# Where VectorE's side work, the maxima's turn and the turns of q and k stand in an attention job

## The reference

```python
for l in range(2):
    proj = x @ w_in[l]
    o_a = chunked attention, 9 chunks of 64 keys, learned relative bias      # 4 heads
    o_b = sliding window of 2 chunks, a learned sink per head                # 4 heads
    o_c = (softmax(s1) - lam * softmax(s2)) @ v, then RMS norm per head      # 4 heads, two maps each
    o_d = attention over the top 256 keys that an indexer chooses            # 4 heads
    x = layer_norm(alpha * x + concat(o_a, o_b, o_c, o_d) @ w_out[l])
    x = layer_norm(alpha * x + square(relu(x @ w_up[l])) @ w_down[l])
```

## Time and profile before

| | us |
|---|---|
| median of 3 runs | 2806.63 (2802.84 to 2807.35) |
| the profiled execution | 2810.08 |
| its span, first to last instruction | 2808.3 |
| TensorE matmuls busy | 2697.7 (96%) |
| VectorE busy | 1670.5 (59%) |
| ScalarE busy | 976.7 (35%) |
| GpSimd busy | 1283.9 (46%) |
| chain that ended last | PE 84%, DVE 10%, DMA 2% |

### The profile page before, as it was taken

How to read it: one execution, slowest core, us unless ns; L and a number is a source line. 1 busy time by engine, 2 the same in 40 slices (tenths; PEclk the granted TensorE clock), 3 DMA queues, 4 the chain that set the end, 5 groups by cost and what they waited for, 6 DMA issues and landing times.

```text
span 2808.3 us, 36228 instructions
## 1 busy us (share of the span) xinstructions
PE 2697.7 (96%) x12768; PEld 2111.0 (75%) x12768; DVE 1670.5 (59%) x3364; ACT 976.7 (35%) x2011; POOL 1283.9 (46%) x1186
## 2 busy tenths in 40 slices
PE   8999999999999999999989999999999999999996
PEld 7788557668788888888777875676787888888885
DVE  3787776635644445544959867766364534345549
ACT  2466444442222212222225655443322222212231
POOL 5433700015665556665555345001156566556562
PEclk9999899999999999999999989999999999999998
DMA  5312334523310111110342132355323111111102
GB/s 153 86 48 56 70 80 90 130 106 94 117 45 20 60 61 61 57 44 27 96 135 55 46 80 47 76 109 117 113 90 106 57 32 32 60 60 60 57 19 101
DMA packets 98570, 207.41 MB, mean 74 GB/s; under 512 B 14138, under 2 KB 23290, under 8 KB 98106
## 3 DMA queue, kind: packets, MB, share of 16 engines
q1 hardware_dynamic: 88952, 177.68, 23.4%
q10 hardware_dynamic: 9440, 27.43, 2.7%
HBM read 142.24 MB, written 8.61 MB: 54 GB/s over the span
## 4 chain that ended last, share of the span: by engine, by line
PE 84%; DVE 10%; DMA 2%; issue 1%; SPq 1%; ACT 1%; ACTq 0%; POOL 0%; DVEq 0%
PE ps L1202 8%; PE ps L1203 8%; PE ps L1204 8%; PE ps L1089 8%; PE ps L1227 7%; PE ps L1226 7%; PE ps L1228 6%; PE ps L882 4%; PE ps L884 4%; PE ps L883 4%; PE ps L1137 2%; PE ps L1135 2%; PE ps L1136 2%; DVE x L1905 1%; PE ps L1031 1%
## 5 line engine op out<-in xcount | busy, mean ns | idle before, releaser
L838 POOL TENSOR_TENSOR wlo<-wraw,whi 128x512 fp32r<-128x512 f32 (+2 forms) x368 | 491.2, 1335 | 249.1 <-ACT whi L1287 227.2
L836 POOL CAST whi<-wraw 128x512 fp32r<-128x512 f32 (+2 forms) x272 | 184.0, 676 | 737.9 <-DMA wraw<-in_w_out 295.1
L1202 PE MATMUL ps<-xhi,whi 128*128 128x512 f32 x1024 | 406.7, 397 | 3.5 <-DVE xlo L1555 3.5
L1203 PE MATMUL ps<-xlo,whi 128*128 128x512 f32 x1024 | 406.6, 397 | 0.0
L1204 PE MATMUL ps<-xhi,wlo 128*128 128x512 f32 x1024 | 406.4, 397 | 0.0
L1976 DVE TENSOR_TENSOR common<-common,ps 128x512 f32<-128x512 f32 x104 | 69.6, 687 | 458.1 <-PE ps L1228 457.6
L1227 PE MATMUL ps<-wlo,op_hi 128*128 128x512 f32 x784 | 311.4, 397 | 0.0
L1226 PE MATMUL ps<-whi,op_hi 128*128 128x512 f32 x784 | 309.4, 395 | 0.0
L1228 PE MATMUL ps<-whi,op_lo 128*128 128x512 f32 x784 | 308.4, 393 | 0.0
L1423 ACT ACTIVATE probT<-ps 128x512 f32<-128x512 f32 (+2 forms) x456 | 204.8, 456 | 251.8 <-PE ps L1060 78.6
L838 POOL TENSOR_TENSOR wlo<-down_raw,whi 128x512 fp32r<-128x512 f32 x168 | 226.0, 1349 | 98.7 <-ACT whi L1287 92.0
(11 more groups left out here) (234 smaller groups left out, 5481.8 us busy)
## 6 DMA issues: line engine op xcount, KB each, us to landing
wraw<-in_w_up SPq DMA_DIRECT2D x144, 256.0 KB, 3.0
down_raw<-in_w_down SPq DMA_DIRECT2D x112, 256.0 KB, 3.6
wraw<-in_w_in SPq DMA_DIRECT2D x80, 256.0 KB, 2.7
slot<-q_part SPq DMA_DIRECT2D x72, 256.0 KB
slot<-k_part SPq DMA_DIRECT2D x72, 256.0 KB
wraw<-in_w_out SPq DMA_DIRECT2D x64, 256.0 KB, 2.8
wraw<-in_w_down SPq DMA_DIRECT2D x32, 256.0 KB, 2.6
slot<-q_part SPq DMA_DIRECT2D x48, 128.0 KB
```

Of the source, the lines that this page charges most:

```text
L838: nc.gpsimd.tensor_tensor(wlo[j][:, 0:w], loaded, whi[j][:, 0:w].bitcast(F32), ALU.subtract).then_inc(S["w_lo"], 1)
L1202: mm(ps[:, b, :], wh, xhi[:, k, tok], start=(k == 0), stop=False)
L1203: mm(ps[:, b, :], wh, xlo[:, k, tok], start=False, stop=False)
```

## The change

It makes four edits.

1. `between` moves from `total - 4` to `total - 3`. In 12-step jobs that is step 9, where VectorE does it behind `take_output`; in B jobs step 6, one step behind the output of step 5.
2. The maxima's turn moves from `total - 3` to `total - 4`, and within a step from the front to a place behind `turn_qk` (TensorE) and `take_turn` (ScalarE), ahead of `turn_out`.
3. A q/k turn may no longer stand at `total - 6` to `total - 4`. The turns then stand as follows (unlisted ones stay): (1,6), (1,10) become (1,10), (2,0); (5,6) becomes (5,10); (7,6), (7,10) become (7,10), (8,0); (8,6), (8,10) become (8,10), (9,0); (10,6), (10,10) become (10,10), (11,0); (11,6), (11,10), (12,0), (12,2) become (11,10), (12,0), (12,2), (12,6); (15,3), (15,7), (16,1) become (15,6), (16,1), (16,3).
4. The squares of C's norm are split: tokens 0 to 511 in job 8 and the rest in job 10, and the root moves from job 10 to job 11.

```diff
 def between_at(n):
     j, g, total = at_step(n)
-    return j + 1 < len(JOBS) and g == total - 4
+    return j + 1 < len(JOBS) and g == total - 3
 def max_turn_at(n):
     j, g, total = at_step(n)
-    return j + 1 < len(JOBS) and g == total - 3
+    return j + 1 < len(JOBS) and g == total - 4
+def pair_turn_allowed(n):
+
+    j, g, total = at_step(n)
+    return not total - 6 <= g <= total - 4 and not {n - TURN_LAG, n + 1 - TURN_LAG} & set(HALF_OF)
...
-            if n >= last + 2 and not max_turn_at(n) and not {n - TURN_LAG, n + 1 - TURN_LAG} & set(HALF_OF):
+            if n >= last + 2 and pair_turn_allowed(n):
...
             for n in range(N_STEPS + LAG):
-                if max_turn_at(n):
-                    turn_max(at_step(n)[0] + 1)
                 if n < N_STEPS:
                     score_t(n)
...
                 if pair_turn_at(n):
                     turn_qk(*pair_turn_at(n))
+                if max_turn_at(n):
+                    turn_max(at_step(n)[0] + 1)
                 if n - TURN_LAG in HALF_OF:
                     turn_out(HALF_OF[n - TURN_LAG])
...
             for n in range(N_STEPS + LAST_STEPS):
-                if max_turn_at(n):
-                    take_max(at_step(n)[0] + 1)
                 if n < N_STEPS:
                     exponent(n)
                 if pair_turn_at(n):
                     take_turn(*pair_turn_at(n))
+                if max_turn_at(n):
+                    take_max(at_step(n)[0] + 1)
...
-                if job == 8:
-                    square_c(0)
-                    square_c(4)
-                if job == 10:
+                if job in (8, 10):
+                    square_c(0 if job == 8 else 4)
+                if job == 11:
                     then(v_.tensor_scalar(ms[:], ms[:], 1.0 / HD, LN_EPS, ALU.mult, ALU.add))
                     rsqrt(ms[:], 32, rs1[:], rs2[:], rsi)
```

## The result

| | before | after |
|---|---|---|
| median of 8 runs each, us | 2808.54 (2802.84 to 2812.02) | 2815.48 (2813.43 to 2816.87) |
| the profiled execution, us | 2810.08 | 2816.87 |
| its span, us | 2808.3 | 2815.1 |

The ratio of the times is 1.0025 with a 95% interval of 1.0016 to 1.0034: the change makes the kernel slower by 6.9 us (4.5 to 9.5). The forecast was 2817.0 us, 10.4 us slower than the median it stood on.

What follows compares the result with a forecast made beforehand. TensorE, busy 96% of the span, was taken as the bound; terms of 4.85 us in the first layer and 5.5 in the second gave +10.4 us, so 2817.0 us against the median 2806.63, range 2803 to 2824.

Steps and rivals of the forecast that it cites:

- The rule that decides: From `turn_out` to the next job's score piece 3, the longer of VectorE's and TensorE's paths sets the time.
- Job 2: Junction after job 2: VectorE needs 5.5 us to piece 3 against TensorE's 4.04, so +1.5 us a layer.
- Job 9: Junction after job 9: VectorE needs 7.0 us to piece 3 against TensorE's 5.23, so +1.8 us a layer.
- Job 0: Junction after job 0: side work can't begin before the output, so piece 3 comes 1.1 us later.
- Job 4: The 1.89 us wait at its step 10 goes; job 5's first turn waits about 0.95: -0.95 us net.
- Job 5 and the stack transfers: Transfers start about 10 us later and meet job 6's maxima row; +0.5 us net, 0.4 more in the second layer.
- Job 8: With one square pair behind the output, the 2.42 us wait at its step 10 goes: -2.4 us.
- B heads: Jobs 12 to 15: waits on the output go, other delays replace them; +2.1 us a layer, bounds -2 and +4.
- The sum: All terms over both attention layers: 4.85 us in the first, 5.5 in the second, together +10.4 us.
- Faster: Side work behind the output finds room on VectorE, so gains stay: 2792 us, or about 2800; chance 0.13.
- No change: B jobs win their 4.4 us minus the copy, junction costs are a third smaller: 2807 us; chance 0.15.
- The late burst costs more: Job 6's maxima wait for the transfers' end and ScalarE holds at job 7: +3 us a layer, 2823; chance 0.12.

Runs made afterwards that it cites:

- side_back: The changed kernel with the side work put ahead of the output again; median 2807.31 us, ratio to before 1.0001.
- the second profile: The changed kernel profiled a second time, with nothing altered; that execution took 2814.89 us.
- squares_only: The kernel before with only the squares split between jobs 8 and 10 and the root in job 11; median 2799.09 us, ratio to before 0.9971.
- side_only: The kernel before with only `between` moved to `total - 3`, behind the output; median 2810.52 us, ratio to before 1.0014.

## Why the forecast held, step by step

- **The rule that decides** (the longer of VectorE's and TensorE's path from `turn_out` to piece 3) held, though of the five waits that were to show 1 to 2 us only those at jobs 6 and 10 do. `nm` waits stand in jobs 1 (0.53), 3 (0.16), 6 and 10, and in the second layer (0.39 us) in job 7; of before the only one that I found at a junction is that of the earlier trace rows, and in side_back none of a microsecond is left. The trace of after shows the sequence at job 9: output from 449.00, side work from 449.56 to 455.02, piece 3 at 455.38.
- **Job 2** was sized too high. The four operations on the bias took 3.56 us before and 2.99 in their new place, so VectorE needed 4.8 us to piece 3 for the 5.5 summed; 0.53 us of wait on `mr` came later in the job, and the block lost 1.0 for 1.5.
- **Job 9** was right at the junction: piece 3 started 6.83 us behind the output's turn (448.55 to 455.38) for VectorE's 7.0 in the forecast, and 5.23 before, so +1.6 for +1.8. The block to job 11 lost only 0.15 to 0.2, or 0.6 with the turn that left, for 1.55. TensorE won 1.0 us back in three places, at the maxima's turns of jobs 10 and 11 and at the turn at (10,10); the forecast had 0.25 of it.
- **Job 0**: priced at +1.1. Piece 3 started 5.57 us behind the output's turn for 4.48 before, which is +1.09; in the second profile it was 4.93, so +0.45, and in the second layer +0.99 and +0.71. The trace says what varies: the small `count` operation. It took 1.01 us from 304.46, and a GpSimd instruction that ran then ended at 305.45, 0.02 us before it. In the second profile it took 0.37 us from 303.40 and ended 0.03 us behind a GpSimd instruction again:

```profile
299.44 0.41 PE L1103 MATMUL ps<-ident_r,oe 65*128 65x65 f32 x4
...
302.46 1.28 POOL L783 TENSOR_TENSOR raw<-raw,cs 128x512 f32<-128x512 f32 x1
...
303.40 0.37 DVE L1816 TENSOR_SCALAR count<-count 128x6 f32<-128x6 f32 x1
...
304.37 0.85 PE L1034 MATMUL ps<-slot 104*128 104x512 f32 x2
```

  The 0.64 us between the two are the whole difference between +1.09 and +0.45. The Trainium skill, "SBUF — State Buffer", Who interferes with whom, says that VectorE in a two-port mode is shut out for a whole GpSimd instruction; these two rows agree with it.
- **Job 4** is the step that failed: a gain was forecast and none came. I had 1.89 us won at (4,10) and 0.95 lost at (5,0); (5,0) lost 2.19. From the output's turn at 358.50 VectorE needs 5.7 us: output, 3.9 us of side work (359.51 to 363.43), the low part. TensorE was at (5,0) at 361.99, after 3.5 us, earlier than the 0.95 allows. With job 5's +0.5 the forecast was -0.45 and -0.75, measured 0.2 to -0.1.
- **Job 5 and the stack transfers**: as told. The burst came 10.05 us later and met job 6's row: 4.79 us from issue to the waiting matmul, against 4.6 forecast (4.02 in the second layer, 4.18 and 4.65 in the second profile). At (7,0) and (7,1) the forecast had VectorE's path as the longer in the first layer. There it was the DMA: 2.10 and 1.49 us of wait on it, and none or 0.24 on `nm`. The whole block from 6 to 9 came within 0.35 us of the sum in either layer. The Trainium skill, "DMA: Bandwidth & Descriptors", Queues, rings and completion order, says that a DMA engine goes round its queues packet by packet. The earlier trace rows has at most 1.9 us for an undisturbed row, so this is the second one that speaks against reading it as the forecast tried to, that a small row slips in at no cost.
- **Job 8**: -2.4 forecast, -2.5 measured in squares_only in either layer, -2.2 and -2.1 in the changed kernel.
- **B heads**: with job 11, 2.3 forecast; measured, less 0.4 for the turn that came over, 3.6 to 4.3. This is the largest miss of the forecast. The waits on the output (4.4 us) went, as told; on the copy (4 times 0.45), on ScalarE (2.6 us, 0.5 before) and on `mr` (1.9) came. Two of these I had at zero: the copy's 0.45 in jobs 13 and 14, taken for covered since `mr` was "only just ready", and the junction 12 to 13, where the side work of job 12 now stands behind the output and piece 3 waits 0.81 us for `nm` (the same wait in either layer):

```profile
500.93 0.39 PE L1036 MATMUL ps<-slot 128*128 128x256 f32 x1 [0.81 <-DVE nm L1757]
```

- **The sum** was 10.4 for 11.6 net of the clock (a term of 0.1 a layer, job 1's side work, was named and not added). The misses in B (+3.2 over both layers) and in jobs 4 and 5 (+1.2) are met by those of jobs 2, 3 and 9 (-3.4), so its closeness is in part luck. The medians moved by 6.9 only, and the forecast has no term for the clock. The four profiles lost 6.8 and 5.1 us to it before, 3.4 and 0 after; 4.3 us of mean difference would bring 11.6 to 7.4, and the counts over all profiles (6.8 and 1.4) would bring it to 6.2. That fits, and is not shown: no run changes the stretches alone.
- **The rivals.** "Faster" needed room behind the output; side_only shows that there was too little. "No change" needed a gain in B; there was a loss. "The late burst costs more" would show as more than 3 us from job 6 to 9; not seen.

## What to carry to other kernels

Before moving work behind a consumer that waits, look for the next consumer in the ring: the one who waits for a PSUM bank, a low part or a copy is found by following VectorE's queue two steps on, and its price is the longer of the two engines' paths, not the idle time of one. Here a late output was cured more cheaply by sharing out the work in front of it (squares in two jobs: 8 us; with one search a job earlier and the smaller edits: 12 us) than by turning the order round. Read a delay as the shift of the instruction against a fixed one before it, not as the wait in its bracket. And a wait of 2 us in the profile may cost 1.7 us more by the clock behind it: profile a kernel twice before reading differences of a few microseconds out of two traces.

## What was not expected of the hardware

- TensorE's granted clock fell to half (1.2 of 2.4 GHz) for 3.4 us at a time, at a single long wait, in a stretch where it is 94% busy: at 360 (1.89 us waited) and 1821 (2.41) of before, 364 (2.19) and 398 (2.10) of after. All 25 such stretches of the eleven profiles, from job 0 on, stand at a wait of 1.67 to 2.83 us. But the same waits passed without it in other executions of the same kernel, so what decides is open.
- A 4 KB transfer on ScalarE's queue took 4.6 us (before, job 5) and 4.8 (after, job 6) from issue to the matmul that waited for it, while SyncE's transfers kept the engines over 90% busy, and 3.5 to 5.5 us over the eleven profiles, against under 2 us alone.
- A VectorE operation on 6 elements a partition took 1.01 us or 0.37 us. Both times it ended 0.02 to 0.03 us behind the GpSimd instruction that it overlapped, and the piece behind it moved by the whole difference.
